# The recurrence of an RWKV-7 and stick-breaking step: K's block moves issued by ScalarE, the load of a moved ahead of B's moves, four weight loads moved behind ScalarE's read of a

## The reference

```python
def _wkv7_scan(S0, r, w, k, v, kk, a):
    # S_t = S_{t-1} (diag(w_t) - kk_t^T (kk_t*a_t)) + v_t^T k_t ;  o_t = S_t r_t
    def step(S, inp):
        r_t, w_t, k_t, v_t, kk_t, a_t = inp
        sa = jnp.einsum("bhvk,bhk->bhv", S, -kk_t)
        S = (S * w_t[:, :, None, :] + sa[..., None] * (kk_t * a_t)[:, :, None, :]
             + v_t[..., None] * k_t[:, :, None, :])
        o_t = jnp.einsum("bhvk,bhk->bhv", S, r_t)
        return S, o_t

def _rwkv7_mix(...):
    ...
    kk = k * k_k; kk = kk / jnp.maximum(norm(kk), 1e-12)
    k = k * (1.0 + (a - 1.0) * k_a)
    o, S = _wkv7_scan(S0, r, decay, k, v, kk, a)
    o = groupnorm(o) * lnx_g + lnx_b + jnp.sum(r * k * r_k, -1) * v
    return (o * silu(g)) @ w_o, ...
```

## Time and profile before

| | us |
|---|---|
| median of 3 runs | 1948.23 (1944.29 to 1948.99) |
| profiled execution, device time | 1941.17 |
| its span, first to last instruction | 1939.4 |
| slots 2 to 14 of the recurrence (530.92 to 754.91) | 223.99 |
| first trunk matmuls to the cache phase (830 to 1000) | 170 |

### The profile page before, as it was taken

The page is one execution under the profiler, slowest core; times in us unless marked ns, Lnnn a source line. Parts: engine busy times, 40 slices in busy tenths (PEclk is TensorE's granted clock), DMA queues, the critical chain, the costliest instruction groups (busy, mean ns, idle before and its releaser), DMA issues.

```text
span 1939.4 us, 44071 instructions
## 1 busy us (share of the span) xinstructions
PE 1799.4 (93%) x18432; PEld 1529.7 (79%) x18432; DVE 1035.4 (53%) x1654; ACT 825.2 (43%) x1555; POOL 262.2 (14%) x331
## 2 busy tenths in 40 slices
PE   7999999999999899999999999999999998777897
PEld 7988999999887788799987676777776776343697
DVE  6744463553688888345445534343463444676334
ACT  4234233233577778433333323333334444555233
POOL 0300000000255566242000000000000000010032
PEclk9999999999999999999999999999999999998899
DMA  8534554555245444244889999999999999999541
GB/s 291 187 141 157 176 179 161 169 172 178 82 112 159 126 135 104 97 147 139 337 302 416 420 419 411 415 426 426 425 426 398 416 426 373 419 382 358 197 147 74
DMA packets 154201, 510.45 MB, mean 263 GB/s; under 512 B 60097, under 2 KB 81986, under 8 KB 108738
## 3 DMA queue, kind: packets, MB, share of 16 engines
q1 hardware_dynamic: 153442, 503.66, 68.7%
q10 hardware_dynamic: 576, 4.19, 0.7%
HBM read 472.86 MB, written 32.32 MB: 260 GB/s over the span
## 4 chain that ended last, share of the span: by engine, by line
PE 32%; DMA 18%; DVE 2%; issue 2%; ACT 1%; SPq 1%; DVEq 0%; ACTq 0%
DMA at_vraw<-in_cache_v 18%; PE psP L2669 8%; PE psP L2670 7%; PE psP L2671 7%; PE at_psO L2723 5%; PE at_psS L2702 3%; SPq L2082 1%; PE psP L2768 0%; PE at_psT L2714 0%; DVE at_o_new L2586 0%; SPq L2122 0%; ACT at_p_w L2389 0%; PE psP L2790 0%; ACT at_p_w L2387 0%; DVE at_w L2519 0%
## 5 line engine op out<-in xcount | busy, mean ns | idle before, releaser
L2669 PE MATMUL psP<-xhi,whi 128*128 128x320 f32 x1488 | 475.5, 320 | 2.9 <-DVE xlo L2556 1.9
L2671 PE MATMUL psP<-xhi,wlo 128*128 128x320 f32 x1488 | 460.7, 310 | 0.0
L2670 PE MATMUL psP<-xlo,whi 128*128 128x320 f32 x1488 | 460.4, 309 | 0.0
L2669 PEld LDWEIGHTS psP<-xhi,whi 128*128 128x128 f32 x1488 | 280.3, 188 | 66.1 <-issue 64.5
L2431 DVE TENSOR_TENSOR wlo<-wraw,whi 128x2048 fp32r<-128x2048 f32 x92 | 212.9, 2314 | 204.9 <-ACT whi L2257 204.7
L2257 ACT ACTIVATE whi<-wraw 128x2048 fp32r<-128x2048 f32 x92 | 176.0, 1913 | 276.3 <-PE psP L2671 275.0
L2670 PEld LDWEIGHTS psP<-xlo,whi 128*128 128x128 f32 x1488 | 280.7, 189 | 0.1
L2671 PEld LDWEIGHTS psP<-xhi,wlo 128*128 128x128 f32 x1488 | 280.2, 188 | 0.0
L139 PE MATMUL psP<-xhi,whi 128*128 128x320 f32 x704 | 218.1, 310 | 2.6 <-DVE wlo L174 2.4
L140 PE MATMUL psP<-xlo,whi 128*128 128x320 f32 x704 | 217.5, 309 | 0.0
L141 PE MATMUL psP<-xhi,wlo 128*128 128x320 f32 x704 | 217.5, 309 | 0.0
(11 more groups left out here) (382 smaller groups left out, 3099.6 us busy)
## 6 DMA issues: line engine op xcount, KB each, us to landing
wraw<-in_weights SPq DMA_DIRECT2D x156, 1024.0 KB, 6.0
at_kraw<-in_cache_k SPq DMA_DIRECT2D x96, 1024.0 KB, 11.2
at_vraw<-in_cache_v SPq DMA_DIRECT2D x94, 1024.0 KB, 10.8
at_kraw<-in_cache_k SPq DMA_DIRECT2D x64, 512.0 KB, 9.8
at_vraw<-in_cache_v SPq DMA_DIRECT2D x62, 512.0 KB, 10.7
rw_s0t<-in_s0T SPq DMA_DIRECT2D x16, 256.0 KB, 3.2
o_wkv_s<-rw_SN SPq DMA_DIRECT2D x16, 256.0 KB, 3.1
wraw<-in_weights ACTq DMA_DIRECT2D x4, 1024.0 KB, 5.5
```

What stands on the lines that cost most here:

```text
L2669: pe.matmul(out, wh, c_.xhi[:, kc, :], start=(kc == 0), stop=False)
L2670: pe.matmul(out, wh, c_.xlo[:, kc, :], start=False, stop=False)
L2671: last = pe.matmul(out, wl, c_.xhi[:, kc, :], start=False, stop=(kc == NM - 1))
```

## The change

Three edits in `recurrence`. `move_blocks` takes the issuing engine as an argument. The four moves of K are now issued by ACT, directly behind its copy into `Kn` and behind a wait of ACT for that copy. The load of a stands on SP ahead of the moves of B and of the wait for ACT's copy `Bn`, no longer behind them; its own wait (`F.g.ka`) stays. ACT's four weight loads stand behind its read of a (`F.a.ka1`), in the same slots.

```diff
+        def move_blocks(eng, x, turned, arrived):
+            for h in range(2):
+                for a_ in range(2):
+                    q, o = L * h + HL * a_, L * h + HL * (1 - a_)
+                    eng.dma_start(x[q:q + HL, :, HL * (1 - a_):HL * (1 - a_) + HL],
+                                 turned[o:o + HL, :, a_]).then_inc(arrived, 16)
...
             def loads_a(t):
-                yield max(AT["F.a.ka1"], AT["F.g.ka"])
+                yield min(AT["F.g.ka"], AT["P.a.Bn"] - 0.0005)
                 F.g.wait(sp, "ka", t)
                 load("a", t + 1)
...
-            def moves(t):
-                for x in sorted("BK", key=lambda x: AT[f"P.a.{x}n"]):
-                    yield AT[f"P.a.{x}n"]
-                    Q.a.wait(sp, x + "n", t)
-                    if x == "B":
-                        move_blocks(Bn[t % 2], BT, b_turned)
-                    else:
-                        move_blocks(Kn[t % 2], KT, k_turned)
+            def moves_of_b(t):
+                yield AT["P.a.Bn"]
+                Q.a.wait(sp, "Bn", t)
+                move_blocks(sp, Bn[t % 2], BT, b_turned)
...
                         Q.a.done(act.activation(flat(x[t % 2][:]), turned[:].rearrange("p c b s -> p (c b s)"), ACT.Copy), name)
+                        if name == "Kn":
+                            Q.a.wait(act, "Kn", t)
+                            move_blocks(act, Kn[t % 2], KT, k_turned)
...
                 elif slot in (4, 6, 8, 10):
-                    yield AT["P.v.Vn"]
+                    yield AT["F.a.ka1"] + 0.0005
                     load_weights(slot // 2 - 2)
```

More of the change, by code:

```diff
@@ L1081, in load_blocks_of_v @@
                         sp.dma_start(VS[q:q + HL], src[:, :, :, a_]).then_inc(vs_in, 16)
[L1083 to L1088, removed]
             def store_gate(grp):
@@ L1179, in _ @@
                              loads_blocks_of_v(p) if 0 <= p < TILES - 1 else none,
-                             moves(p) if 0 <= p < TILES else none,
+                             moves_of_b(p) if 0 <= p < TILES else none,
                              stores_wkvp(u) if 0 <= u < TILES else none, stores_wkv(u) if 0 <= u < TILES else none,
```

## The result

The changed kernel takes 1981.45 us (median of 4 runs, 1979.44 to 1984.58) against 1947.69 us before (median of 4, one more than ahead of the prediction): a ratio of 1.0178, 95% interval 1.0158 to 1.0197. It is slower by 1.8%; 1984 was forecast. The profiled execution has a span of 1978.5 us, 39.1 more than before. By the medians the distance is 33.8 us, because the profiled execution before was 7.1 us under its median and this one 1.2.

What follows compares the result with a forecast made beforehand. The recurrence was taken as the bound, its short slots paced by ACT. Stall 40.0 + clock 19.6 - a's lateness 24.1 = +35.5 us on 1941.2, plus 7.1 to the runs' median: 1984, range 1958 to 2008.

Steps and rivals of the forecast that it cites:

- The stall: ACT between its copy Kn and D4t: issuing K's moves delays D4t 2.6 us a slot, 40.0 us together.
- K's issues back up: Rival, chance 0.06: both engines issue at once, groups take up to 4.25 us, each slot loses 1.7 more: 2009 us.
- plain slot: Recurrence slot without a's lateness: the short slot of 15.72 us less 0.47 of waiting for a, 15.25 us.
- The clock: PE's idle time before Y halves its clock, costing 1.4 us more in each of slots 2 to 15: 19.6 us.
- a's lateness: ACT's waits for the load of a make recurrence slots long; issuing a earlier was to gain 24.1 us.
- price of nothing for B's later moves: B's moves on SP, issued up to a microsecond later behind a, cost nothing: their reader S0 is in the next slot.
- Faster: Rival, chance 0.09: ACT's stall is absorbed by later waits; 1940 us with 1.6 a slot absorbed, 1924 with all hidden.
- the two later waits: ACT's waits later in a short slot: 0.81 us for DVE's state and 0.79 for PE, forecast to absorb nothing.

Runs made afterwards that it cites:

- e6: Kernel before with only the load of a moved ahead of B's moves; K's moves on SP, weight loads at the slots' end: 1927.5 us, ratio 0.9903.
- e5: Changed kernel plus five idle matmuls on PE before Y in each slot but the first: 1969.0 us, ratio 1.0109 to the kernel before.
- e10: e6 with each 1 MB weight load split into four of 256 KB, two a slot near its end: 1924.1 us, ratio 0.9893 to the kernel before.
- e2: Changed kernel with K's moves back on SP, the edits to a and the weights kept: 1932.9 us, ratio 0.9942 to the kernel before.
- e9: Kernel before with only the weight loads moved behind ACT's read of a; a behind B's moves: 1939.3 us, ratio 0.9976.
- e11: e2 run once more, beside e10 on one chip: 1929.1 us, ratio 0.9942 to the kernel before.
- e8: Changed kernel with two of K's four moves back on SP, the first two staying on ACT: 1949.1 us, ratio 1.0009 to the kernel before.
- e3: Changed kernel with K's moves on ACT in two later pairs, behind the copy of B and behind O2: 1935.0 us, ratio 0.9947 to the kernel before.
- e12: Changed kernel with K's four moves on ACT in one later group, behind the copy of B: 1939.4 us, ratio 0.9960 to the kernel before.
- e4: Changed kernel plus eight idle matmuls on PE before Y in each slot but the first: 1977.3 us, ratio 1.0174 to the kernel before.

## Why the prediction was right, and where its terms were off

**The stall** was right in place, mechanism and price. 2.6 us were forecast between the copy and D4t, 2.65 are there in the row above; the idle time before Y is there in 12 of the 13 slots and is put down to D4t (in slot 8 PE comes late to Y for another idle time). In four of the 13 slots the group took over 3 us, so that the mean wait is 37.7 / 13 = 2.9. The rival "K's issues back up" had such groups, of up to 4.25, but not for its reason: while these four were being issued (542.82 to 546.65 is the longest), SP issued nothing. Why they took longer stays open. A small part of the stall is given back: the plain slot grew from 15.5 (e6) to 17.8, by 2.3.

**The clock** came out near the forecast sum by two errors. 14 falls at 1.4 us, 19.6, were forecast. In slots 2 to 14 there were 8, besides the one at the start of slot 2 that the kernel before has too, and one more in slot 15; from slot 9 on they come in every second slot. Where two neighbouring slots differ in nothing else, one costs 1.95 us (19.71 and 17.76), which makes 17.6 for the nine. e5 shows that this loss is real.

**a's lateness** is the term that was mis-sized. 24.1 us were to come back. In the profiled slots a alone brings 12.6 (223.99 to 211.43), with the smaller weight loads 17.5, with the change's own place for the weights 9 to 11. Two steps of the working failed. The plain slot was set at 15.72 less the 0.47 us of waiting, 15.25, but it is 15.5 to 15.6: PE alone is busy 15.1 to 15.2 us in it (e10), as it was before. And the surplus of all long slots was booked on a, while a weight load of 1 MB stretches a slot without a as well, through idle times by issue where it stands behind the read of a (e2) and through B's moves where it stands at the slot's end (e6). The changed kernel has 4.9 us of the first kind and none of the second, so the prediction's price of nothing for B's later moves held there. Moving the weights was taken as pure gain; e9, and e2 beside e6, show no gain. The prediction also read the long slots wrongly in one point: it says that in the four longest a weight load had just been issued. That is so for those of 21.75 and 20.85 us. In those of 18.39 and 18.27 ACT waits for a as well (1.63 and 1.71 us), but the weight loads come only at their end, at 581.39 and 616.15.

**What of it was lucky**: two errors cancelled. With the changed kernel's own place for the weights the a term was too good by 13 to 15 us. Beside e2 and e11, in which only K's moves differ, slots 2 to 14 became 40.2 and 42.4 us longer, where the stall and the clock had been given 13 x (2.6 + 1.4) = 52.0, so these two were too dear by 10 to 12. What is left is a difference of 3 us in these slots (27.9 forecast, 31.1 measured). The other slots had 7.6 in the forecast and have 8.0, of which 2 are there before the change can act.

**The rivals.** "Faster" was given 1.6 us a slot as its deciding point, and this rested on the 24.1 of a: e8, with a stall of 1.33, should have won by it and is level. Its reason ("absorbed by the two later waits") fails for issues in front of D4t; issues that stand right ahead of those waits, as in e3, are hidden. The prediction said that ACT does nothing during an issue, from one row. For a group behind a wait for ACT's own last result that holds; as a general statement e3 and e12 refute it. The rule on spreading DMAs over engines that can issue them, from the Trainium skill (Perfetto Trace Analysis, section DMA Optimizations), was set against the rows for this receiver. By e3 there is a place on ACT at which the issues cost nothing that the time shows, and still nothing is gained over e2 (0.9947 and 0.9942): with a moved ahead, taking K's moves off SP was worth nothing.

## What to carry to other kernels

Before moving DMA issues to a compute engine, look at what stands directly ahead of them: behind a wait for that engine's own last result they cost their full issue time (0.6 us each for these small ones), and whatever waits for the next instruction pays it too, with the clock on top. A few instructions later, ahead of a wait that the engine has anyway, they were nearly free. When a queue is full and one transfer in it is late, first move that one transfer ahead; here this alone was worth 1%. Then look at what now stands behind it: B's moves became late as soon as a large load ran beside them. And test the edits of a bundle one by one: of these three one gained, one did nothing measurable and one lost more than twice the gain.

## What the runs showed of the hardware

- DMA issues on ACT run ahead of activations that stand before them in the program, by about a microsecond in e12 (751.83 against 752.83), unless they wait for ACT's own result (758.55 behind 758.52 in the changed kernel).
- PE's clock did not follow each idle time. Of the longest idle times in each of slots 2 to 14 of the changed kernel (2.1 to 3.7 us), eight were followed by 3.41 us at half clock and five by none. The longest without a fall was 2.87 us, the shortest with one 2.37. Before the change the two longest idle times (2.8 and 3.6 us) had 6.82 us behind them; none of these had.
- In most versions with the load of 1 MB behind the read of a, PE has idle times of 1.0 to 3.2 us with no releaser that end 7 to 9 us after such a load is issued, at instructions that recur (the first D2t products, the second S1 product). It is not a rule: of the four loads e3 has it behind each, the changed kernel behind two, e5 behind one and e4 behind none. With 256 KB pieces near the slot's end (e10) the longest is 0.3 us.
- A move of 32 x 5 x 32 numbers takes 2.3 us to land in the median of e6, but up to 6.3 us beside a load of 1 MB; beside loads of 256 KB it took at most 4.0 (e10).
